# Moving the closings of attention blocks, some weight splits and two waits, and turning the output to token-major form, in a three-layer network on one core

## The reference, cut to what matters

```python
def swa_layer(h, k, v, positions, norm_w, in_w, q_norm_w, sinks, out_w):
    u = rms_norm(h, norm_w)
    q, gate = jnp.split(u @ in_w, 2, axis=-1)
    q = rope(rms_norm(q.reshape(b, s, ATT_HEADS, HEAD_DIM), q_norm_w), positions)
    o = swa_sink_attention(q, k, v, sinks)
    return (o * jax.nn.silu(gate)) @ out_w
...
        x = x + conv_ffn(rms_norm_2(x, ln2_g[i]), w_up[i], conv_w[i], conv_b[i], w_down[i])
        gate = jax.nn.sigmoid(rms_norm_2(x, ple_norm_g[i]) @ w_ple_gate[i])
        x = x + gate * (p[i].astype(x.dtype) @ w_ple_proj[i])
    return rms_norm_2(x, final_g)
```

## Time and profile before

| | |
|---|---|
| median of 3 runs | 1473.22 us (1473.07 to 1475.22) |
| the profiled execution's own time | 1473.84 us |
| its span | 1472.0 us |
| PE busy | 1405.7 us, 95% |
| DVE / ACT / POOL busy | 845.0 / 647.1 / 509.1 us |
| mean granted TensorE clock | 0.976 |

### The profile page before, as it was taken

How to read it: one execution, slowest core, us unless ns; L and a number is a source line. 1 busy time by engine, 2 the same in 40 slices (tenths; PEclk the granted TensorE clock), 3 DMA queues, 4 the chain that set the end, 5 groups by cost and what they waited for, 6 DMA issues and landing times.

```text
span 1472.0 us, 18153 instructions
## 1 busy us (share of the span) xinstructions
PE 1405.7 (95%) x6802; PEld 1106.8 (75%) x6802; DVE 845.0 (57%) x1444; ACT 647.1 (44%) x1092; POOL 509.1 (35%) x257
## 2 busy tenths in 40 slices
PE   7999999999999999999999999998999999999996
PEld 5767778777778777667887888675557888888785
DVE  5576555756567755774687022456656654554655
ACT  5654525445355533674654212344444333232452
POOL 2563544536210100465000334224343555555200
PEclk9999999999999999999999999989999999999998
DMA  5221223222222223201233334020002333333321
GB/s 180 87 71 58 86 72 86 58 72 72 86 72 86 86 86 86 86 16 55 89 104 111 100 121 137 29 72 29 16 15 72 87 100 101 94 92 101 113 88 57
DMA packets 33366, 118.92 MB, mean 81 GB/s; under 512 B 3964, under 2 KB 4348, under 8 KB 33024
## 3 DMA queue, kind: packets, MB, share of 16 engines
q1 hardware_dynamic: 31680, 113.26, 25.0%
q10 hardware_dynamic: 1600, 4.50, 0.9%
HBM read 115.65 MB, written 2.10 MB: 80 GB/s over the span
## 4 chain that ended last, share of the span: by engine, by line
PE 86%; DVE 5%; ACT 5%; issue 2%; POOL 1%; ACTq 0%; DVEq 0%
PE bank L1201 82%; PE bank L1598 1%; PE bank L1452 1%; ACT arena L1137 1%; ACT wsh L824 1%; DVE arena L1726 1%; POOL wsl L676 1%; DVE arena L2100 1%; DVE arena L1745 0%; DVE wsl L1655 0%; PE bank L1320 0%; PE bank L1354 0%; ACT arena L873 0%; DVE arena L2224 0%; ACTq L767 0%
## 5 line engine op out<-in xcount | busy, mean ns | idle before, releaser
L676 POOL TENSOR_TENSOR wsl<-ring,wsh 128x1024 fp32r<-128x1024 f32 x136 | 328.9, 2419 | 630.4 <-ACT wsh L824 630.4
L824 ACT ACTIVATE wsh<-ring 128x1024 fp32r<-128x1024 f32 x199 | 210.6, 1058 | 543.0 <-PE bank L1201 498.9
L1201 PE MATMUL bank<-parts1h,wsh 128*128 128x512 f32 x728 | 292.8, 402 | 19.9 <-DVE parts1l L1679 10.5
L1201 PE MATMUL bank<-parts0h,wsh 128*128 128x512 f32 x704 | 284.8, 405 | 7.8 <-DVE wsl L1655 3.3
L1201 PE MATMUL bank<-parts1l,wsh 128*128 128x512 f32 x728 | 286.2, 393 | 0.0
L1201 PE MATMUL bank<-parts1h,wsl 128*128 128x512 f32 x728 | 286.2, 393 | 0.0
L1201 PE MATMUL bank<-parts0h,wsl 128*128 128x512 f32 x704 | 276.2, 392 | 0.0
L1201 PE MATMUL bank<-parts0l,wsh 128*128 128x512 f32 x704 | 276.1, 392 | 0.0
L1201 PEld LDWEIGHTS bank<-parts1h,wsh 128*128 128x128 f32 x728 | 138.4, 190 | 54.0 <-DVE wsl L1655 10.5
L1201 PE MATMUL bank<-arena 128*64 128x128 f32 (+9 forms) x964 | 164.0, 395 | 13.7 <-DVE small L2224 5.6
L1201 PEld LDWEIGHTS bank<-parts0h,wsh 128*128 128x128 f32 x704 | 133.2, 189 | 45.6 <-issue 13.2
(11 more groups left out here) (287 smaller groups left out, 1855.8 us busy)
## 6 DMA issues: line engine op xcount, KB each, us to landing
ring<-in_wstream SPq DMA_DIRECT2D x210, 512.0 KB, 3.6
arena<-in_alibi ACTq DMA_DIRECT2D x2, 1024.0 KB, 5.0
outT<-arena SPq DMA_DIRECT2D x8, 256.0 KB, 2.1
h<-in_xT SPq DMA_DIRECT2D x2, 512.0 KB, 7.4
h<-in_xT ACTq DMA_DIRECT2D x2, 512.0 KB, 8.0
arena<-in_cmpb ACTq DMA_DIRECT2D x1, 496.0 KB
con<-in_con ACTq DMA_DIRECT2D x1, 390.5 KB
rowb<-in_rowb ACTq DMA_DIRECT2D x1, 184.0 KB
```

The costliest lines, as they stand in the source:

```text
L676: return nc.gpsimd.tensor_tensor(dst, src, hi.bitcast(F32), ALU.subtract)
L824: nc.scalar.activation(wsh[n % NSET][:, :], src, ACT.Copy).then_inc(*done("high", ("high", L)))
L1201: return nc.tensor.matmul(*args, **kw)
```

## The change: what it does

- In `pipeline` a closing is moved behind the scores S of the unit three ahead. The sparse attention's `nO` goes wholly behind S and R. The sliding-window closing is divided: `aO` (DVE's gating) goes behind S, `aP` (ACT's rounding and POOL's subtraction) behind R.
- `psp 1` moves from behind gate 7 to behind the second unit's V. Gate 7 keeps only its tanh on ACT; DVE forms (tanh + 1) times the bank, and a new step `half` halves it on ACT behind `psp 1`.
- Two spans of DVE splits end earlier: at gate 0 (11 splits of steps gate 1 to q 1 3 go to POOL), and at `cmp_in 0` (2 splits go to POOL).
- `sout` and `dn` wait for the tiles of their input one by one.
- The end becomes token-major: PE multiplies each 128 x 128 piece of h with a diagonal of the final gains (formed by ACT at `psp 2`). The pieces of tiles 0 to 3 are multiplied between `ple 2 4` and `ple 2 5`, those of 4 and 5 between `ple 2 6` and `ple 2 7`, tile 6 in `norm 7`, tile 7 in `last`. ACT copies the first halves to SBUF. When the root is there, DVE scales four of them and ACT the four others, with one number for each token. The diagonal of roots and its broadcast are gone. DVE, not ACT, squares the last tile. The host turns the output accordingly.

```diff
@@ pipeline
-        if i and units[i - 1] in closing:
-            out.append((x + "O", *units[i - 1]))
+        closes = i and units[i - 1] in closing
         if i + 3 < n:
             out.append((x + "S", *units[i + 3]))
+        if closes and x == "a":
+            out.append(("aO", *units[i - 1]))
         if i + 2 < n:
             out.append((x + "R", *units[i + 2]))
+        if closes:
+            out.append(("aP" if x == "a" else "nO", *units[i - 1]))
         out.append((x + "V", *u))
@@ steps
-    out += [("gate", 6)] + swa[:7] + [("gate", 7), ("psp", 1), ("qT", 1)]
+    out += [("gate", 6)] + swa[:7] + [("gate", 7), ("qT", 1)]
...
+    k = body.index(("aV", *units[1])) + 1
+    out += body[:k] + [("psp", 1), ("half",)] + body[k:]
...
-    out += [("ple", 2, m) for m in range(KD)]
-    out += [("norm", 7), ("nb", 7), ("hn", "final")]
+    out += [("ple", 2, m) for m in range(5)] + [("turn", 0), ("ple", 2, 5), ("ple", 2, 6), ("turn", 1), ("ple", 2, 7)]
+    out += [("norm", 7), ("last",)]
@@ on_vector
-    spans = [(("sout", 3, 0), ("q", 1, 3)), (("ao", 1, 0), ("mv", 0)), (("dn", 3, 0), ("ple", 2, KD - 1))]
+    spans = [(("sout", 3, 0), ("gate", 0)), (("ao", 1, 0), ("cmp_in", 0)), (("dn", 3, 0), ("ple", 2, KD - 1))]
@@ ScalarE
+                if step == ("turn", 0):
+                    for t in range(NT):
+                        act.wait_ge(*at("mm", "fin", t, 0))
+                        nc.scalar.activation(res[:, 2 * t, :], ps(("fin", t, 0))[:, :], ACT.Copy)\
+                            .then_inc(*done("final_act", ("turned", t), ("free", "fin", t, 0)))
+                if k == "last":
+                    act.wait_ge(*at("rinv"))
+                    for t in range(NT):
+                        act.wait_ge(*at("mm", "fin", t, 1))
+                        nc.scalar.activation(res[:, 2 * t + 1, :], ps(("fin", t, 1))[:, :], ACT.Identity, scale=nrm[:, 1, t:t + 1])\
+                            .then_inc(*done("final_act", ("result", 2 * t + 1)))
...
-                        link(nc.scalar.activation(gs[:, a[0], :], ps(step)[:, :], ACT.Tanh, scale=0.5))
-                        nc.scalar.activation(gs[:, a[0], :], gs[:, a[0], :], ACT.Identity, scale=0.5, bias=halfone[:, 0:1])\
-                            .then_inc(*done("gtanh", ("gtanh",)))
+                        nc.scalar.activation(gs[:, a[0], :], ps(step)[:, :], ACT.Tanh, scale=0.5).then_inc(*done("gtanh", ("gtanh",)))
+                if k == "half":
+                    act.wait_ge(*at("gdouble"))
+                    nc.scalar.activation(gs[:, KD - 1, :], gs[:, KD - 1, :], ACT.Copy, scale=0.5).then_inc(*done("gs", ("gs", KD - 1)))
@@ TensorE
+                def turned(half, m):
+                    pe.wait_ge(*at("h", 7, m))
+                    for t in range(NT):
+                        last = mm(ps(("fin", t, half))[:, tok(m - 4 * half)], h[:, m, tok(t)], wdiag[:, m, :], start=True, stop=True)
+                        if m in (3, KD - 1):
+                            last.then_inc(*done("mm", ("mm", "fin", t, half)))
...
-                    if m == 0:
-                        for q in range(GT):
-                            pe.wait_ge(*at("yn", g, q))
-                    quarter(step, ("sout", g, m // 2), xg, 0, m)
+                    quarter(step, ("sout", g, m // 2), xg, 0, m, lambda kt: ("yn", g, kt))
...
-                    if m == 0:
-                        pe.wait_ge(*at("ff", 4 * q + 3))
-                    quarter(step, ("dn", q, m // 2), xg, 4 * (q % 2), m)
+                    quarter(step, ("dn", q, m // 2), xg, 4 * (q % 2), m, lambda kt: ("ff", 4 * q + kt))
@@ VectorE
+                if k == "last":
+                    dve.wait_ge(*at("rinv"))
+                    for t in range(NT):
+                        dve.wait_ge(*at("turned", t))
+                        nc.vector.tensor_scalar(res[:, 2 * t, :], res[:, 2 * t, :], nrm[:, 1, t:t + 1], None, ALU.mult)\
+                            .then_inc(*done("final_dve", ("result", 2 * t)))
...
-                    nc.vector.tensor_tensor(gs[:, a[0], :], gs[:, a[0], :], ps(step)[:, :], ALU.mult)\
-                        .then_inc(*done("gs_dve", ("gs", a[0]), ("free", *step)))
+                    nc.vector.scalar_tensor_tensor(gs[:, a[0], :], gs[:, a[0], :], 1.0, ps(step)[:, :], ALU.add, ALU.mult)\
+                        .then_inc(*done("gs_dve", ("gdouble",), ("free", *step)))
```

More of the change, by code:

```diff
@@ L286, in jobs_of @@
         return [(k, *a[:-1], t) for t in range(NT)] if a[-1] == 0 else []
+    if k == "turn":
+        return [("fin", t, a[0]) for t in range(NT)]
     if k == "kT":
@@ L947, in _ @@
                         nc.scalar.activation(xgh[:, m, :], xs[g % 2][:, m, :], ACT.Copy).then_inc(*done("ynhi", ("ynhi", g, m)))
+                if k == "psp" and a[0] == 2:
+                    for m in range(KD):
+                        last = nc.scalar.activation(wdiag[:, m, :], ident, ACT.Identity,
+                                                    scale=vec[:, V_NORM["final"] + m:V_NORM["final"] + m + 1])
+                    last.then_inc(*done("final_act", ("wdiag",)))
                 if k == "pp":
@@ L962, in _ @@
                     nc.scalar.activation(gsig[m % 2], gsig[m % 2], ACT.Sigmoid).then_inc(*done("gsig", ("gsig", i, m)))
-                    if m == KD - 1:
-                        square(2 * i + 2 if i < 2 else 7, m)
+                    if m == KD - 1 and i < 2:
+                        square(2 * i + 2, m)
+                    if m == KD - 1 and i == 2:
+                        link(nc.scalar.activation(tiny[:, :], eps[:, :], ACT.Sqrt))
                 if k == "sines":
@@ L1229, in linear, with quarter @@
                 last.then_inc(*used(name, ("mm", *job)))
-            def quarter(job, name, src, lo, m):
+            def quarter(job, name, src, lo, m, ready=None):
                 b = open_bank(job)
@@ L1235, in quarter @@
                 for kt in range(4):
+                    if ready and m == 0:
+                        pe.wait_ge(*at(*ready(kt)))
                     last = mm3(b[:, :], [q[:, kt * 256 + (m % 2) * P:kt * 256 + (m % 2 + 1) * P] for q in w],
@@ L1266, in _ @@
                 k, a = step[0], step[1:]
+                def turned(half, m):
[4 more added lines that the diff above has]
+                            last.then_inc(*done("mm", ("mm", "fin", t, half)))
+                if k == "turn":
+                    pe.wait_ge(*at("wdiag"))
+                    for t in range(NT):
+                        open_bank(("fin", t, a[0]))
+                    for m in ((0, 1, 2, 3), (4, 5))[a[0]]:
+                        turned(a[0], m)
+                if step == ("norm", 7):
+                    turned(1, 6)
                 if k == "norm":
@@ L1426, in _ @@
                 if k == "gate":
-                    linear(step, blocks_of(step)[0], hn, None if a[0] else "attn")
+                    linear(step, own_blocks(step)[0], hn, None if a[0] else "attn")
                 if k == "aS":
@@ L1719, in _ @@
                         for m in tiles_of(a):
-                            if m >= 4 and ver < 7:
+                            if m >= 4:
                                 dve.wait_ge(*at("hn", name, m - 4))
@@ L1729, in _ @@
                                                            ALU.mult, ALU.mult)\
-                                .then_inc(*done("hf", ("result", m) if ver == 7 else ("hf", name, m),
+                                .then_inc(*done("hf", ("hf", name, m),
                                                 *([("accfree", "rb", ver)] if m == KD - 1 and name != "kv" else [])))
-                            if ver < 7 and m % 2:
+                            if m % 2:
                                 dve.wait_ge(*at("hnhi", name, m - 1))
```

26 lines of the change are left out of this document (17 added, 9 removed).

## The result

The changed kernel takes 1447.97 us (median, 1447.3 to 1448.72) beside 1473.14 for the kernel before in the same comparison: a ratio of 0.9826, 95% interval 0.9809 to 0.9844, 25.2 us less. Two repeats gave ratios of 0.9819 [0.9767, 0.9872] and 0.9821 [0.9791, 0.9851].

The account below looks back on a forecast made before the run. PE bounds the kernel, busy 1405.7 of 1472.0 us, so only its 66 us of standing still or its work matter. Terms sum to -15.0 from 1473.84, giving 1458.8, stated as 1458.5 for the median; range 1451 to 1466.

Parts of the forecast that it names:

- the price of the clock: Half-clock stretches behind four waits: only part comes back, -1.5 (sparse attention), -0.6 (Mamba output) and -0.5 us (sliding window).
- Rival 2: The clock comes back everywhere: all four stretches at full clock, 8.5 us in place of 2.6, 1452.6 us; chance 0.07.
- Sparse closings: Sparse attention: DVE masks first, so PE's three waits for score banks (5.6 us) go, less 0.2 each for restarts: -5.0.
- Query splits: Query stage: low parts made on POOL are ready before the step ends, removing two PE waits of about 1.6: -3.2 us.
- Gate 7: Sliding-window attention: query copies come 1.6 us earlier, PE waits 1.8 for them; work returns behind unit 1: -1.2 (bounds -0.3, -3).
- rival 1: Both attentions: the next wait is right behind, so the attention terms are lost: -5.8 us, 1467.5; chance 0.15.
- Sliding-window closings: Sliding-window attention: POOL's subtraction moves behind the scaling PE waits 2.1 us for, which starts 1.0 earlier: -1.0.
- The end: Kernel's end: six tiles of added products cost +5.3 us, scaling starts 2.8 earlier: together +2.5 (bounds +1 and +5).
- Rival 3: The end costs its full price, +5.3 us and no gain: 1461.3; its chance is within the forecast's 0.73.
- Rival 4: Slower: DVE's two-input operations hold POOL's 13 moved splits, PE stands 1.2 us at each: 1479; chance 0.03.
- What would show it: PE's waits at 2224, 1655 and split tiles gone or under 1 us, L739 near 1; second column sums some 12 earlier.
- three signs of a wrong prediction: PE idle falls under 12 us; DVE rotation rows of 2 us delay scores; stores start no earlier after the last product.

## Why the prediction was right or wrong

**The step that failed: the price of the clock.** The sum took the four stretches of the earlier trace rows, gave back a part of each, and came to 1.5 + 0.6 + 0.5 = 2.6. It was 10 to 14. Two things were wrong. *The share.* I took 0.3 to 0.5 of the stretches behind the waits, arguing that small matmuls keep the clock down; all four are gone in all three profiles of the changed kernel, and both of theirs in the one with the three mask waits filled (4.4 of 5.1). Rival 2, with 8.5 for the clock, was nearer. *The list.* I counted only stretches right behind removed waits. The earlier trace rows was chosen out of twelve. Between 925 and 1008 (us of before) the changed kernel has 20.5, 13.7 and 23.9 us of half clock in its three profiles, before 27.3 and 23.9 in its two.

How far a stretch hangs on its wait can be counted over the 20 profiles of this study:

| half clock at (us of before) | profiles with the wait as before | profiles with it closed, moved or filled |
|---|---|---|
| 410, behind the Mamba wait | 8 of 8 | 0 of 12 |
| 1042, behind the second mask wait | 8 of 8 | 0 of 12 |
| 1076, behind the third | 5 of 8 | 0 of 12 |
| 615, behind gate 7 | 6 of 10 | 0 of 10 |
| 653, behind a sliding-window closing | 4 of 8 | 0 of 12 |
| the feed-forward's pair of waits | 8 of 16 | 0 of 4 |

Two of the four stretches of the earlier trace rows thus belong to their wait. The other two come in about half of the profiles when nothing is changed there, so the one profile that the forecast was made from was unlucky in them, and the change gets credit for taking away what would often not have been there. Half clock is not fixed by the program, as the second profile of before shows. What I should have done is to bound the term by all twelve, 58.0 / 2 = 29.0, and widen the range downwards. (By its own steps the sum gives 1458.2 and not 1458.5.) Why the whole gets 13.7 by the clock while its parts alone get 2 to 3.5 each (together 15.0, the end's 3.5 among them) is not settled. The sum fits, but even kernels whose edit only fills waits or only turns the end have 2 to 3.5 less than before. Some of that is the yardstick: the mean of before by the clock is 31.3 to 35.6 from comparison to comparison. Against the before of their own comparison the parts get 1.4, 2.5, 2.1, 2.7 and 1.8, together 10.5, the two repeats of the whole 14.7 and 14.0, and the two kernels that only fill waits 3.9 and 0.9.

**At full clock the sum was nearly right, by errors that cancel:** forecast -15.0 + 2.6 = -12.4, measured -12.8.
- *Sparse closings*, forecast -5.0: -8.4 alone, +8.9 undone. The waits were the right ones, and so was the order behind the change. The term was mis-sized because I took the idle time for the price of a wait and 0.2 off it. PE's timeline before, around (a product with float32 operands has two records, so x2 is one of four score products):

```profile
1038.75 0.91 PE L1201 MATMUL bank<-arena 64*128 64x384 f32 x2
...
1044.05 0.79 PE L1201 MATMUL bank<-parts0h,wsh 128*128 128x512 f32 x1
```

  and the same eight products after:

```profile
1017.88 1.56 PE L1227 MATMUL bank<-arena 64*128 64x384 f32 x8
1019.37 0.50 PE L1227 MATMUL bank<-parts0h,wsh 128*128 128x512 f32 x1
```

  From the first of the eight to the block product it was 5.30, and is 1.49. Take off 0.98 for the clock (half of 1044.05 - 1042.10) and 2.83 is left, for a wait shown as 1.86. The same sum gives 2.9 at the first closing (shown as 1.94) and 3.2 at the third (1.78): 8.9 in all. The first closing, where no half clock disturbs it, shows what the idle time leaves out. Before, then after:

```profile
1009.64 0.70 PE L1201 MATMUL bank<-arena 64*128 64x256 f32 x2
1012.28 1.39 PE L1201 MATMUL bank<-arena 64*128 64x256 f32 x6 [1.94 <-DVE small L2224]
```

```profile
997.70 1.14 PE L1227 MATMUL bank<-arena 64*128 64x256 f32 x8
```

  The six records behind the wait take 1.39, more than all eight without it. The trace has the start of each: after, they come in pairs (0, 0.01, 0.32, 0.33, 0.54, 0.54, 0.75, 0.76 from the first), so two products of 64 rows run side by side; before, one by one (0, 0.32, 2.64, 2.96, 2.98, 3.30, 3.33, 3.65). The wait falls between the two products of a pair: the first runs alone for 0.70, and only from its end is the idle time counted. Why the products behind the wait don't pair either is not shown.
- *Query splits*, forecast -3.2: -3.8 in both profiles and in the part alone. Here too the idle time is too small a price: large products start every 0.23 and their rows say 0.39, and the start behind the wait (2.02 behind the last) is followed by one 0.31 later, so each wait, shown as 1.63, costs 2.02 - 0.23 + 0.08 = 1.9.
- *cmp_in and mv*, -1.7: -2.1. *Mamba output*, -2.0: -2.0 and -2.1. *Feed-forward output*, -0.8: -1.7 to -1.8 (by block 0.3 at each of three earlier groups, too short to stand in the earlier trace rows, and 1.1 at the last).
- *Gate 7*, forecast -1.2: not there. From 594 to 642 the changed kernel is at -0.4 where kernels with neither edit nor the stretch at 615 are at -1.3, that is 0.9 worse; undone, it is 0.6 better, within the uncertainty. The sum itself named the risk, work coming back behind unit 1 "with unit 2's copies queued behind", and left it inside a slack of about 1. The timeline of PE after shows where the query copies' 1.8 went:

```profile
605.72 0.65 PE L1227 MATMUL bank<-arena 128*64 128x256 f32 x4 [0.67 <-ACT arena L1056]
610.05 1.09 PE L1493 MATMUL bank<-con,arena 128*128 128x128 f32 x8 [1.24 <-POOL arena L745]
614.26 0.65 PE L1227 MATMUL bank<-arena 128*64 128x256 f32 x4 [1.37 <-DVE arena L2096]
```

  The third of these waits has its cause in the timelines. DVE's split of `p` before; then after, with the copy behind it that PE waits for; then POOL's scaling after:

```profile
613.47 1.30 DVE L1655 TENSOR_TENSOR parts0l<-ring,parts0h 128x1024 fp32r<-128x1024 f32 x1 [0.26 <-ACT parts0h L819]
```

```profile
611.12 2.48 DVE L1696 TENSOR_TENSOR parts0l<-ring,parts0h 128x1024 fp32r<-128x1024 f32 x1 [0.57 <-ACT parts0h L825]
613.52 0.68 DVE L2096 COPY arena<-bank 128x512 f32<-128x512 f32 x1
```

```profile
610.63 1.89 POOL L745 TENSOR_TENSOR arena<-arena,small 128x1024 f32<-128x1024 f32 x1 [0.64 <-DVE small L2088]
```

  The sum had 1.3 for this split. At its new place it starts while POOL scales, takes 2.48, ends 1.08 behind POOL's end at 612.52, and the copy comes 1.2 later for it: nearly all of the 1.37 that PE waits, and as much as the term. All three profiles of the changed kernel have the 2.48 and the 1.37; with gate 7's part undone the split takes 1.31 again and PE's wait for the copy is gone. It is the lock of the earlier trace rows, whose bound of 2.4 the sum gave to the query stage only. The next wait was right behind, as in rival 1, here and only here. *Sliding-window closings*, -1.0: -1.4 and -1.3.
- *The end*, +2.5: +1.8 and +1.4 by the shifts (from -28.3 to -26.5, from -31.4 to -30.0), +2.4 alone. `turn 0` took its 3.6 exactly. From the second sums 9.8 were left, forecast 10.5. Priced at full clock it is 4 to 5, since the old end's extra time lay half in a tail at half clock. Rival 3 (full price) was not the case.

**The rivals.** Rival 4, POOL's splits held by DVE, did not come, and the lock it rests on did, the other way round. Besides the split of `p`, it is to be seen after in the rotations (the timeline of DVE, then that of POOL at the same time):

```profile
518.28 0.42 DVE L2041 TENSOR_TENSOR arena<-arena 128x256 f32<-128x256 f32 x1
...
519.61 2.54 DVE L2041 TENSOR_TENSOR arena<-arena 128x256 f32<-128x256 f32 x1
```

```profile
519.47 2.40 POOL L682 TENSOR_TENSOR wsl<-ring,wsh 128x1024 fp32r<-128x1024 f32 x1 [13.61 <-ACT wsh L830]
```

The same operation takes 0.42 and, beside POOL's split, 2.54: it ends 0.28 behind POOL's end at 521.87. The Trainium skill (SBUF — State Buffer, section "SBUF: two separate sides") says that one engine holds the shared ports for the whole instruction; the trace agrees. The 0 that the sum took for it in the query stage was right, as no PE wait names these rotations; behind gate 7 it was not.

**What would show it:** lines 2224 and 1655 and both split tiles are gone from PE's waits; L739 is at 2.4, not near 1, so the sliding-window part shortened a wait of 2.1 and left three of up to 1.2; the second sums start 1458.64 - 1435.73 = 22.9 earlier, where 12 were forecast, and nearly all of that difference of 11 is the clock again. Of the three signs of a wrong prediction none came: PE's idle time fell by 18.6, the slow rows of DVE in the rotations made PE wait for nothing, and the stores start 2.5 behind the column sums, where it was 6.2.

## What to carry to other kernels

Split a kernel's time by the mean clock first: the part at full clock repeats with a deviation of 1.6 us where the time itself ran from 1465 to 1486, and a small gain can be read from it. Price a wait of PE from the start of the last product ahead of it to the start of the next, less the products' normal distance (nearly nothing where two run side by side), not by the idle time: here 2.8 for 1.86. Before moving work of DVE, look at what POOL does at the new place. And bound the clock's part of a forecast by all of the half-clock time around the touched stages, not by the stretch behind each wait; it can come back in full, and another can appear where nothing was touched.

## What the runs showed of the hardware that I had not expected

- One program's half clock differs between executions: 58.0 and 64.9 us ahead of the end in two profiles, (1 - clock) x span from 23 to 46 in 82 executions, at a time at full clock of 1439.4 with a deviation of 1.6. The Trainium skill (TensorE: Matmul & The Clock Gate, section "Part 1: The HAM clock gate (the "warmup" mystery)") says of a kernel's start that the number of slow products differs from run to run; these runs show the same for stretches in the middle. It puts the penalty of a start under 1% of a typical span; here the slow stretches over the whole span can have cost 32.9 of 1472, 2.2%.
- Half clock can be nearly free: 6.8 us of it in the sliding-window attention cost 1.3 us, while 10.2 us of it on the feed-forward's full products cost 4.9 (the shift goes from -31.6 to -26.7).
- A wait between two products of 64 rows that run side by side without it cost 2.8 to 3.2 where its idle time was 1.8 to 1.9, and the six records behind it took 1.39 where eight took 1.14.
- A float32 transpose of 128 x 128 took half of what the product with a diagonal took: the pieces of `turn 0` in 1.91 us against 3.73.
